# Expert weight blocks in seven and eight buffers that go round, in place of six in pairs

## What is computed

```python
    y = jnp.zeros((m, d), jnp.float32)
    for e in range(N_EXPERTS):
        hid = jax.nn.silu(x2 @ w_gate[e]) * (x2 @ w_up[e])
        y = y + combine[:, e:e + 1] * (hid @ w_down[e]).astype(jnp.float32)
```

## Time and profile before

| | us |
|---|---|
| median of 3 runs | 1469.57 |
| lowest, highest | 1468.09, 1473.25 |
| profiled execution, its device time | 1469.94 |
| its span | 1468.2 |
| PE busy in the span | 1318.9 (90%) |
| first layer's expert stage (PE, from the first gate to the last down) | 393.7 to 687.4 |
| second layer's | 1142.0 to 1433.4 |

### The profile page before, as it was taken

One profiled execution on the slowest core, in us unless ns is written; L12 is line 12 of the kernel. 1 busy time (PEld: TensorE's weight loads), 2 busy tenths in 40 slices (PEclk: granted clock), 3 DMA queues, 4 the chain that ended last, 5 costly groups with the idle time before them and its releaser, 6 DMA issues. The chain is left out here.

```text
span 1468.2 us, 27307 instructions
## 1 busy us (share of the span) xinstructions
PE 1318.9 (90%) x10905; PEld 741.6 (51%) x10906; DVE 577.3 (39%) x1435; ACT 304.2 (21%) x783; POOL 185.4 (13%) x469
## 2 busy tenths in 40 slices
PE   7999999999599999887899998889995999998990
PEld 3444456544365456554643444556543655555550
DVE  2159944443423111111658995665216131111115
ACT  2121144411100000001213215555302000000002
POOL 1010092010100000001203661000101000000002
PEclk9999999999699999998799999899998899999995
DMA  9541489934587999999301133332514589999966
GB/s 283 193 132 58 147 315 314 340 123 131 182 324 264 393 376 403 405 409 359 105 0 58 33 115 116 116 116 73 216 72 174 196 320 366 397 391 402 403 268 205
DMA packets 87597, 341.06 MB, mean 232 GB/s; under 512 B 25843, under 2 KB 33107, under 8 KB 73506
## 3 DMA queue, kind: packets, MB, share of 16 engines
q1 hardware_dynamic: 67466, 289.49, 52.7%
q0 software_dynamic: 10656, 37.56, 7.3%
q10 hardware_dynamic: 9344, 12.20, 2.4%
HBM read 309.09 MB, written 30.47 MB: 231 GB/s over the span
## 5 line engine op out<-in xcount | busy, mean ns | idle before, releaser
L1265 PE MATMUL banks<-arena 128*32 128x128 f32 (+1 forms) x4736 | 358.2, 334 | 26.7 <-issue 13.7
L1265 PEld LDWEIGHTS banks<-arena 128*32 128x32 f32 (+1 forms) x4736 | 238.9, 126 | 145.3 <-issue 52.5
L1293 PE MATMUL banks<-arena 128*64 128x512 f32 (+1 forms) x1184 | 173.1, 492 | 1.1 <-ACT arena L1755 1.1
L1861 DVE TENSOR_TENSOR arena<-arena,banks 128x256 f32<-128x256 f32 (+5 forms) x84 | 38.5, 459 | 272.1 <-PE banks L1265 176.8
L940 PE MATMUL banks<-arena 128*128 128x512 f32 x320 | 141.1, 595 | 1.2 <-DMA arena<-in_wstream 1.1
L2233 DVE COPY arena<-banks 128x256 f32<-128x256 f32 (+1 forms) x56 | 21.4, 382 | 295.8 <-PE banks L1278 289.5
L1861 DVE TENSOR_TENSOR arena<-banks,arena 128x512 f32<-128x512 f32 (+5 forms) x159 | 70.6, 473 | 124.4 <-ACT arena L1677 84.5
L1168 PE MATMUL banks<-arena 128*128 128x512 f32 x256 | 115.6, 610 | 3.6 <-ACT arena L1795 2.3
L968 PE MATMUL banks<-arena 128*128 128x512 f32 x256 | 116.5, 600 | 0.0
L1755 ACT ACTIVATE arena<-banks 128x512 f32<-128x512 f32 (+1 forms) x56 | 29.6, 528 | 363.2 <-PE banks L1293 363.2
L1293 PEld LDWEIGHTS banks<-arena 128*64 128x64 f32 (+1 forms) x1184 | 58.6, 123 | 84.4 <-issue 70.0
(11 more groups left out here) (292 smaller groups left out, 1429.2 us busy)
## 6 DMA issues: line engine op xcount, KB each, us to landing
arena<-in_wstream SPq DMA_DIRECT2D x109, 2048.0 KB, 14.7
arena<-in_fox_kt SPq DMA_DIRECT2D x64, 256.0 KB, 4.5
arena<-in_fox_v SPq DMA_DIRECT2D x64, 256.0 KB, 4.2
arena<-in_dsa_page SPq DMA_DIRECT2D x64, 256.0 KB, 4.1
expert_rows<-arena ACTq DMA_DIRECT2D x76, 128.0 KB, 9.2
expert_rows<-arena POOLq DMA_DIRECT2D x1, 6656.0 KB, 20.5
hn_scratch<-arena POOLq DMA_DIRECT2D x8, 512.0 KB, 3.0
expert_rows<-arena ACTq DMA_DIRECT2D x68, 32.0 KB, 7.7
```

The lines of the kernel that those rows point to most:

```text
L1265: last = mm(bank(b, 0, 4 * n, n * j, n * j + n), x[:, c, :], w[:, c, 4 * n * j:4 * n * j + 4 * n], start=(c == 0), stop=(c == DC - 1))
L1293: last = mm(bank(3, 0, 8 * n, n * q, n * q + n), ht2[g % 2][:, 128 * i + n * j:128 * i + n * j + n], w[:, c, 8 * n * q:8 * n * q + 8 * n], ...
L1861: return v.tensor_tensor(out, x, y, op)
```

## The change

Expert blocks no longer belong to a parity. Block n goes to place n mod 7 in the first layer and n mod 8 in the second. The new seventh place is `WORK` 0 to 4095, the eighth `QT` 0 to 4095 (second layer only). Block n waits for block n-7 (or n-8) to be used up, and blocks 6 (and 7 in the second layer) wait for no block. Because the norm's rows lie in the seventh place, SP waits for both `hn_out` semaphores behind `ranked`. The load of `wtail1` waits for the last user of the seventh place. Some semaphores are merged (`lf_dve` and `lf_act` to `lf`; `ln_var`, `ln_root`, `ln_done` to `ln`) with the same waits.

```diff
+SLOTS = (7, 8)
...
-    slots = [[[ring[2], ring[0], ring[1]], over_w], [[ring[1], ring[2], ring[0]], over_w]]
+    slots = [[ring[i] for i in first] + over_w + [at(*wide) for wide in more]
+             for first, more in (((2, 0, 1), [("WORK", 0, 4096)]), ((1, 2, 0), [("WORK", 0, 4096), ("QT", 0, 4096)]))]
...
+    def slot_of_block(l, s, i):
+
+        return slots[l][(3 * s + i) % SLOTS[l]]
+
+    def block_landed(l, s, i):
+
+        n = 3 * s + i
+        return f"weights{l}_{n % SLOTS[l]}", 16 * (n // SLOTS[l] + 1)
+
+    def block_used(l, s, i):
+
+        before, j = divmod(3 * s + i - SLOTS[l], 3)
+        name = ("gate_mm", "up_mm", "down_mm")[j] + str(l)
+        return name, upto(name, ENDS[before])
...
             sp.wait_ge(S(f"ranked{l}"), upto(f"ranked{l}", 1))
+            sp.wait_ge(S(f"hn_out{l}_0"), upto(f"hn_out{l}_0", 48))
+            sp.wait_ge(S(f"hn_out{l}_1"), upto(f"hn_out{l}_1", 32))
             for s in range(2, NE):
                 k = sp.value_load(block_i[0:1, s:s + 1], min_val=0, max_val=3 * NE - 3)
-                for i, name in enumerate((f"gate_mm{l}", f"up_mm{l}", f"down_mm{l}")):
-                    sp.wait_ge(S(name), upto(name, ENDS[s - 2]))
+                for i in range(3):
+                    if 3 * s + i >= SLOTS[l]:
+                        name, count = block_used(l, s, i)
+                        sp.wait_ge(S(name), count)
                     sp.wait_ge(S("x_in_0"), 16)
                     weights(l, s, i, a["wstream"][bass.ds(k + (b + i), 1)].rearrange("a p w -> (a p) w"))
...
-        sp.wait_ge(S("row_u0"), 1)
+        sp.wait_ge(S("down_mm0"), upto("down_mm0", ENDS[13]))
         sp.dma_start(at("WORK", 3072, 576), a["wtail1"]).then_inc(S("c_late"), 16)
```

More of the change, by code:

```diff
@@ L121 @@
     (64, "vnew"),
-    (128, "xg weights"),
+    (128, "xg"),
 )
@@ L125 @@
 PER_PARITY = {"hn_out": (48, 32), "yb": (16,) + (32,) * (NT - 1),
+              "weights": tuple(16 * len(range(i, 3 * NE, SLOTS[0])) * (i < SLOTS[0]) for i in range(max(SLOTS))),
               "y_rows": tuple(max(STORED[i::4]) for i in range(4))}
@@ L532, in weights @@
         def weights(l, s, i, src):
-            sp.dma_start(slots[l][s % 2][i], src).then_inc(S(f"weights{l}_{3 * (s % 2) + i}"), 16)
+            sp.dma_start(slot_of_block(l, s, i), src).then_inc(S(block_landed(l, s, i)[0]), 16)
         def first_weights(l, s, i):
@@ L560, in experts @@
                 index_keys(0, 12)
-                sp.wait_ge(S("ln_done"), 1)
+                sp.wait_ge(S("ln"), 3)
                 first_weights(0, 1, 0)
@@ L1271, in landed @@
             def landed(s, i):
-                pe.wait_ge(S(f"weights{l}_{3 * (s % 2) + i}"),
-                           upto(f"weights{l}_{3 * (s % 2) + i}", 16 * (s // 2 + 1)))
+                name, count = block_landed(l, s, i)
+                pe.wait_ge(S(name), upto(name, count))
             def turn_hid(g):
@@ L1288, in down @@
                     pe.wait_ge(S(f"y_ev{l}"), upto(f"y_ev{l}", g))
-                w = g3(slots[l][s % 2][2], 4)
+                w = g3(slot_of_block(l, s, 2), 4)
                 for c in range(4):
@@ L1305, in experts @@
                     pe.wait_ge(S(f"silu{l}"), upto(f"silu{l}", g))
-                part_features(0, g3(slots[l][s % 2][0], DC), x, n).then_inc(S(f"gate_mm{l}"), 1)
+                part_features(0, g3(slot_of_block(l, s, 0), DC), x, n).then_inc(S(f"gate_mm{l}"), 1)
                 if g > 0:
@@ L1314, in experts @@
                     pe.wait_ge(S(f"ht_ev{l}"), upto(f"ht_ev{l}", g - 1))
-                part_features(1 + g % 2, g3(slots[l][s % 2][1], DC), x, n).then_inc(S(f"up_mm{l}"), 1)
+                part_features(1 + g % 2, g3(slot_of_block(l, s, 1), DC), x, n).then_inc(S(f"up_mm{l}"), 1)
                 if g == ENDS[s] - 1 and s + 1 < NE:
@@ L1394, in beside_even @@
                 if t == 0:
-                    pe.wait_ge(S("lf_dve"), 1)
+                    pe.wait_ge(S("lf"), 1)
                 pe.wait_ge(S("u_ready"), t + 1)
@@ L1616, in project_even @@
                 if job == 10:
[L1617 to L1620, removed]
+                    act.wait_ge(S("lf"), 1)
+                    af(lf_tmp[0], lf_tmp[0], ACT.Exp).then_inc(S("lf"), 1)
+                    act.wait_ge(S("lf"), 3)
+                    af(lf_tmp[0], lf_tmp[0], ACT.Ln).then_inc(S("lf"), 1)
                 if 12 <= job < 22:
@@ L1790, in _ @@
         af(tick[0], tick[0], ACT.Sqrt)
-        act.wait_ge(S("ln_var"), 1)
-        af(lnv, lnv, ACT.Sqrt).then_inc(S("ln_root"), 1)
-        act.wait_ge(S("ln_done"), 1)
+        act.wait_ge(S("ln"), 1)
+        af(lnv, lnv, ACT.Sqrt).then_inc(S("ln"), 1)
+        act.wait_ge(S("ln"), 3)
         for c in range(4):
@@ L2346, in _ @@
         v.scalar_tensor_tensor(out=lf_tmp[0], in0=lf_tmp[1], scalar=-1.0, in1=lf_tmp[1], op0=ALU.mult, op1=ALU.min)\
-            .then_inc(S("lf_dve"), 1)
+            .then_inc(S("lf"), 1)
         step(v.tensor_scalar(lf_tmp[2], lf_tmp[1], 0.0, None, ALU.min))
@@ L2358, in new_logf @@
         def new_logf():
-            dve.wait_ge(S("lf_act"), 1)
-            v.tensor_scalar(lf_tmp[0], lf_tmp[0], 1.0, None, ALU.add).then_inc(S("lf_dve"), 1)
+            dve.wait_ge(S("lf"), 2)
+            v.tensor_scalar(lf_tmp[0], lf_tmp[0], 1.0, None, ALU.add).then_inc(S("lf"), 1)
         def split_logf():
-            dve.wait_ge(S("lf_act"), 2)
+            dve.wait_ge(S("lf"), 4)
             tt(lft, x3[2], x3[0], ALU.subtract).then_inc(S("logf"), 1)
@@ L2433, in layer_norm @@
             v.tensor_scalar(lnv[:, 0:SEQ], bank(7), 1e-5, None, ALU.add)
-            v.tensor_scalar(lnv[:, SEQ:TOK], bank(6, 0, 64), 1e-5, None, ALU.add).then_inc(S("ln_var"), 1)
-            dve.wait_ge(S("ln_root"), 1)
+            v.tensor_scalar(lnv[:, SEQ:TOK], bank(6, 0, 64), 1e-5, None, ALU.add).then_inc(S("ln"), 1)
+            dve.wait_ge(S("ln"), 2)
             step(v.reciprocal(lnv, lnv))
             tt(xt[:, 0:4, 0:SEQ], conv_p, bc_mid(lnv[:, 0:SEQ], 4), ALU.mult)
-            tt(xt[:, 0:4, SEQ:TOK], conv_s, bc_mid(lnv[:, SEQ:TOK], 4), ALU.mult).then_inc(S("ln_done"), 1)
+            tt(xt[:, 0:4, SEQ:TOK], conv_s, bc_mid(lnv[:, SEQ:TOK], 4), ALU.mult).then_inc(S("ln"), 1)
         attend(0, 4, lambda t: causal[:, 384 - 128 * t:512])
```

## The result

The changed kernel takes 1451.23 us (median, 1450.28 to 1451.78) against 1471.26 for the kernel before in the same comparison (its earlier runs had 1469.57). The ratio is 0.9875, 95% interval 0.9853 to 0.9898, that is 15 to 22 us less, with 18.4 in the middle (the two medians lie 20.0 apart). The profiled execution has a span of 1450.0 us against 1468.2.

The account below looks back on a forecast made before the run. The prediction held PE and the weight stream both close to the bound, the late half in step with the stream. It summed 1469.94 - 6.2 (first layer) - 11.9 (second) = 1451.8, said 1452 us, with an 8-in-10 range of 1444 to 1462.

Parts of the forecast that it names:

- What bounds the kernel: Expert stages: PE and the weight stream are both close to the bound; better block supply can give at most 29.0 us.
- How a place acts: Expert stages: each added place issues a block when the block before was issued, so the stream's unbroken run starts earlier.
- The first layer, -6.2: First layer, one place more: blocks 16 to 47 land 6.2 us earlier, late waits stay; -6.2 us of 15.9.
- rival B: Weight stream: blocks cost more in the longer unbroken run; part of gain lost, chance 0.11, or slower than before, 0.05.
- The second layer, -11.9: Second layer, two places more: block 16 lands 11.9 us earlier, all waits go but the last 1.2 us; -11.9 us.
- None does now: Second layer: of the 34 blocks from block 16 on, none finds an empty queue after the change, as before.
- Blocks 6 and 7 give nothing by themselves: Early loads: issued some 17 us earlier, but wanted only by expert 2, so no gain of their own.
- The gather: Start of the stage: block 6's data start when the first gather is in, so meeting it costs 0.
- rival C: First gather meets block 6 (and 7): PE's wait grows up to 6.9 us in each layer, 1466; chance 0.07.
- Rival A: All block waits go in both layers, needing 5.39 instead of 5.74 us a block: -29.0, 1441; chance 0.08.
- Rival B in full: Weight stream dearer until slower than before by over 0.3%; at 358 GB/s, 0.79 us more a block, +25 us; chance 0.05.
- The rest: SP's queue and semaphores: `wtail1`'s wait, the merged semaphores, SP's later waits and value reads cost 0.

## Why the prediction was right

The time, 1452 for 1451.2, and the range held, and so did the mechanism. That they agree within 1 us is luck: both terms were sized too high, 18.1 us in all where the stage lengths give 14.5, and the four runs of the first result were low ones for this kernel (1455.38 when run again, which the range holds too).

- *What bounds the kernel* held. With the stream's time cut, both stages fall to 277 us without a wait: all that a better supply can give was put at 29.0 us and is about 30 by this measure (291.9 + 292.2 - 276.9 - 277.1). Two readings on the way were wrong and change nothing: the five waits of the second layer sum to 11.4 (13.1 is with the slow group), and block 26 did not find the queue empty before, since block 25 landed 2.0 us after its issue.
- *How a place acts* held: the block that starts the unbroken run is issued when the one or two before it used to be (in the first layer block 15 where 14 was; in the second block 16, 75.7 us into the stage, where block 14 was at 75.6), and from there on the DMA engines are busy throughout. What was mis-sized is the lead that this gives. The prediction took it in microseconds, where the run starts, and carried it unchanged to the last waits. The landings show that it is kept in blocks instead. They are counted here from the stage's first gate and averaged over the two to seven traces that tell them, which are not the same ones for each block, so a lead is good to about 1 us (the differences are taken before rounding):

| landing, us after the first gate | six places | more places | earlier by |
|---|---|---|---|
| first layer, block 15 | 90.7 | 85.3 (seven) | 5.4 |
| first layer, block 22 | 132.0 | 127.4 | 4.6 |
| first layer, block 34 | 206.3 | 200.5 | 5.9 |
| first layer, block 41 | 245.8 | 241.2 | 4.6 |
| second layer, block 20 | 121.3 | 108.4 (eight) | 12.8 |
| second layer, block 22 | 132.4 | 121.4 | 11.1 |
| second layer, block 44 | 261.8 | 251.9 | 9.9 |

In the second layer block 22 lands with eight places when block 20 does with six (121.4 and 121.3), and block 45 when block 43 does (256.7 and 257.3). By this a place is worth what one block takes where PE waits last, some 5 us here, and not what the first block of the run gained.

- *The first layer, -6.2.* Block 15's landing 6.8 us earlier, no empty queue after it, the wait at block 19 gone, those at experts 11 and 14 kept (6.35 us, where about 9 had been forecast). The landings give some 5 us all along and the stages 4.4 over seven traces, 8.7 in the one pair. A part of what is too much is that the trace of before was a late one at block 15 (91.3 us into the stage, 90.0 and 90.7 in two others). The stream's step a block is not to blame: from block 27 to block 41 it is 5.92 to 6.08 us with seven places and 5.96 to 6.00 with six, so rival B does not show here.
- *The second layer, -11.9.* "None does now" held: block 22 has block 21 before it, and the engines are busy. At block 20 the blocks were 12.8 us earlier, even more than forecast; at block 22 they are 11.1 and at block 44 9.9 us earlier, and the stages give 10.0. Two us go at block 21, which takes 7.3 and 7.5 us with eight places and 5.0 and 5.3 with six. The third line of the stretches in the result, 308 GB/s beside a gather and stores, is of that block; that these cost it the time is not shown by a run. Left over at expert 14 are 4.5 us, not 1 or 2.
- *Blocks 6 and 7 give nothing by themselves*: shown, by the kernel that holds them back. *The gather* (rival C): the first gather is not touched in either layer. The second one was, 10.5 us instead of 4.6, which I had not named; it has some 9 us to spare.
- *Rival A* (all waits go) did not come with the old order. It came with the new order of experts, at an unchanged stream, and its price of 29 was right (29 to 31 measured). My condition for it, a cheaper block, was one of two ways; I had not seen that the order of the rooms could do it.
- *Rival B in full*, by the Trainium skill's 358 GB/s ("DMA: Bandwidth & Descriptors", on where 436 GB/s comes from): the run without a gap is longer now, and it holds 397 GB/s over 160 us in one layer and 156 in the other. The trace does not agree with that rule for a core that runs alone:

```profile
480.00:640.00 160.00, 154.63 (x1638) 90.20 (x1636) 21.06 (x50) 13.52 (x31) 8.21 (x9) 0.99 1.01 397
1244.00:1400.00 156.00, 151.07 (x1711) 88.73 (x1709) 19.91 (x48) 13.60 (x31) 6.39 (x7) 1.00 1.01 397
```

- *The rest*, the added waits for the norm rows, `wtail1` and the merged semaphores: the kernel with six and six places has them all and stands within 0 to 7 us under the kernel before, so they cost nothing that shows.

## What to carry to other kernels

When a stream of weights and a matrix engine need about the same time, look for the last block that found the queue empty: from there on each further buffer lets the stream run one block further ahead, and it is worth about what one block takes where the engine waits last (4 to 6 us here), not what the first block gains. Before buying buffers, look at the order of the work: large pieces together leave the stream idle, small pieces together make the engine wait, and mixing them gave as much here (1452.5 with six places) as one and two more buffers (1451 to 1455), and both together 1441. And look at what a transfer that the next stage waits for has before it in its queue: here some 9 us between the stages may come from a store behind prefetches, which no run tried by itself.

## What the runs showed that I had not expected

Whether the clock drops after a wait is not settled by the wait's length here. In the kernel with six and six places a wait of 1.89 us was followed by a slow group, with a granted clock of 0.68 over its 5.36 us, so partly at the lower of the two levels, 1.2 GHz. In the changed kernel a wait of 3.50 was followed by one at full clock, 1.00 or 2.4 GHz (its row stands above, at 1375.54), and in the kernel before one of 3.59 as well (at 647.24):

```profile
1289.36 5.36 PE L1287 MATMUL banks<-arena 128*64 128x256 f32 x32 [1.89 <-DMA arena<-in_wstream]
```

A slow group costs 1.3 to 1.7 us more than the 3.67 it should take, and in five traces one cost 2.7 to 2.9 (6.39 to 6.61 us). A stage of six or seven places has none to two of them, so stages of equal waits differ by that, which can be a part of the scatter between runs.
